# Natural-order normalised rows with strided TensorE transposes, and the last weight split of each attention half placed behind its softmax

## The chip, the cores and the metric

The kernel runs on one core of one Trainium2 chip. The metric is device time in microseconds (us) from the start to the end of one execution; the median of several executions is quoted. Everything is one launch, with all arithmetic on the core.

## What is computed

Two pre-norm residual layers over 512 tokens of width 1024, in float32. Each layer is a token mixer (layer 0 a gated short convolution, layer 1 attention with three dilated windows and rotary positions) followed by a mixture of 16 experts. Cut to what the change touches:

```python
hn = rms_norm(h, norm_mix[i])                      # y = x * rsqrt(mean(x*x) + eps) * g
h = h + mixer(hn)                                  # layer 0: conv, layer 1: attention
hn = rms_norm(h, norm_ffn[i])
h = h + hierarchical_moe(hn, ...)                  # top-1 of 4 groups, then top-2 of 4 experts
# expert e:  silu(t @ w_gate[e]) * (t @ w_up[e]) @ w_down[e]
return rms_norm(h, norm_final)
```

## The kernel before

**Tiles.** The 512 tokens stand in `h` as four row tiles `r` of 128 tokens (partitions) by 1024 channels. A product needs the channels on the partitions, so every normalised row tile is turned by TensorE into eight 128x128 tiles (`k` = 0 to 7) in PSUM. Tile `k` holds the channels 8q + k, q being the partition, because the weights are loaded with the pattern `(p k) n -> p k n`: partition p then reads eight neighbouring rows of the weight matrix in one piece.

**Precision by splitting.** Each operand is split into a high part (ScalarE copies it to the type fp32r) and a low part (VectorE subtracts the high part from the original), and each product is three matmuls, hi*hi, hi*lo and lo*hi (`product`, L298 to L300). Weights come as units of 1 MB. The projections outside the experts use three landing buffers `raw` and two pairs `W_hi`/`W_lo`; in ScalarE's code `hi(u)` (L592) and in VectorE's code `lo(u)` (L816) split unit `u`. The experts use six landing buffers `m_raw` and three pairs (L623, L982).

**Stages on TensorE.** `turn_rows` (L1275) turns the four normalised row tiles, 4 x 8 transposes. It runs four times: before the convolution's projections, before the router of layer 0, before attention's projections, and before the router of layer 1. Around it VectorE runs `norm_row` (L849: hn = h * rstd * gain) and `turn_lo` (L855), ScalarE runs `square` (L598) and `turn_hi` (L603), and GpSimd makes rstd (L470, L471). `norm_row` is used a fifth time for the output.

**Experts.** The normalised rows are also stored to the DRAM tensor `hn_rows`. For each expert item (a block of up to 128 tokens of one expert) GpSimd gathers 128 rows into `x_rows`, `turn_x` (L1348) turns them with eight transposes, and then come four gate/up units of 12 matmuls each and two down units of 12. `turn_x(i + 1)` stands between the gate/up and the down units of item i.

**The permutation.** In the kernel before, `norm_row` writes hn with its channels permuted: it reads `h` and `gain` at a step of eight elements and writes `hn` in one piece, so that the columns of tile k lie side by side:

```python
o = hn[r % 2][:, :].rearrange("p (k q) -> p k q", k=KD)
i0 = h[:, r, :].rearrange("p (q k) -> p k q", k=KD)
rows = hn_r[r % 2][:, k * P:(k + 1) * P]           # turn_rows, and x_rows_r alike in turn_x
```

`pe.transpose(out, rows, ident_r)` loads `rows` as the stationary operand (the row PEld in the profile is this load) and streams the identity.

**Attention.** Two halves `s` of eight heads each. A half projects q, k and v of three head groups `g` (units 0 to 5 of each group, `p` = 0, 1, 2 for q, k, v), and then `attend(s)` runs 16 units `u` (four pairs of heads by four query tiles): scores on TensorE (L1471, L1474), mask and row minimum on VectorE (L1161), exponential on ScalarE (L729), transposes of the probabilities (L1486), their copy back (L1173), weighted sum (L1500). Behind the 16 units VectorE computes the merge scales (`scales`, L1180 to L1190), with one ScalarE exponential in the middle (L762); in half 1 TensorE spreads them (L1454) between the row tiles of the output projection's first unit, VectorE merges (L1199 to L1201) and splits (L1206), and the projection's second unit waits for the last of these splits.

**Order.** Every engine's order is written out by hand. Splits run two units ahead, so while TensorE runs the last unit of group 2, ScalarE and VectorE have one split left to do, `hi(U_QKV + 7)` and `lo(U_QKV + 7)`. It can't begin before TensorE has left the buffer, and in the kernel before it stands right ahead of `attend(s)` on both engines. SyncE issues all weight loads in one queue; a load waits for the low split that frees its buffer.

Of the kernel before, what the change touches and what calls it, by code (L numbers as in the profile page):

```python
# [23 lines left out]
ALU = mybir.AluOpType  # L24
# [32 lines left out]
def build(nc, x, positions, norm_mix, norm_ffn, norm_final, conv_w_in, conv_w, conv_w_out, attn_w_qkv,  # L57
# [19 lines left out]
    with ExitStack() as ctx:  # L77
# [85 lines left out]
        stat_sum = keep("stat_sum", [P, 2, NT, 8])  # L163
        head_scale = keep("head_scale", [P, 2, NT, 8])
        cos_t = keep("cos_t", [P, NT, HD])
        sin_t = keep("sin_t", [P, NT, HD])
# [160 lines left out]
        def _(sp):  # L327
# [95 lines left out]
            store_rows(4)  # L423
            norm_gain(2)
            for j in range(3):
                qkv_unit(j, 0, 0)
            later_weights(0)
            y_back(0)
# [159 lines left out]
        def _(act):  # L588
# [161 lines left out]
            def attend(s):  # L750

                act.wait_ge(qkT_ready, s * 24 + 24 + 4)
                softmax_exp(0, s)
                for u in range(16):
                    if u + 1 < 16:
                        softmax_exp(u + 1, s)
                    if u % NT == 0 and u:
                        store_heads(u // NT - 1, s)
                    if s == 1 and u in (2, 6):
                        heads_hi(u // 4)  # L760
                act.wait_ge(gap_in, s + 1)
                act.activation(stat_exp[:, :, :, :], stat_exp[:, :, :, :], ACT.Exp).then_inc(gap_out, 1)  # L762
                store_heads(3, s)

            for s in range(2):
                for g in range(NATT):
                    for p in range(3):
# [13 lines left out]
                        if p == 2:  # L781
                            for r in range(NT):
# [6 lines left out]
                                else:  # L789
                                    act.activation(v_all[:, g, r, :], ps[:, r, :], ACT.Copy).then_inc(v_ready, 1)  # L790
                        hi(U_QKV + 2 * p + 3, rev)
                attend(s)
# [12 lines left out]
        def _(dve):  # L805
# [26 lines left out]
            def norm_row(k, first, r):  # L832
# [3 lines left out]
                if r >= 2:  # L836
# [4 lines left out]
                    if first == 16:  # L841
                        dve.wait_ge(out_stored[r % 2], 16)
                if first < 16:
                    o = hn[r % 2][:, :].rearrange("p (k q) -> p k q", k=KD)
                    i0 = h[:, r, :].rearrange("p (q k) -> p k q", k=KD)
                    i1 = gain[:, :].rearrange("p (q k) -> p k q", k=KD)
                else:
                    o, i0, i1 = hn[r % 2][:, :], h[:, r, :], gain[:, :]
                dve.scalar_tensor_tensor(out=o, in0=i0, scalar=rstd[:, r:r + 1], in1=i1, op0=ALU.mult,  # L849
                                         op1=ALU.mult).then_inc(hn_ready, 1)  # L850

# [358 lines left out]
            def attend(s):  # L1210

                dve.wait_ge(qkT_ready, s * 24 + 24 + 4)
                mask_scores(0, s)
                for u in range(16):
                    if u + 1 < 16:
                        mask_scores(u + 1, s)
                    probs_back(u, s)
                    if s == 1 and u in (4, 8):
                        heads_lo(u // 4 - 1)
                scales(s)  # L1220

            def rope(g4, rev, p):
# [14 lines left out]
            for s in range(2):  # L1237
                for g in range(NATT):
                    for p in range(3):
# [4 lines left out]
                        if p < 2:  # L1244
                            rope((s * 6 + g * 2 + p) * 4, rev, p)
                        lo(U_QKV + 2 * p + 3, rev)
                        if s == 1 and g == 0:
# [20 lines left out]
        def _(pe):  # L1268
            def turn_rows(first):

                for r in range(NT):
                    pe.wait_ge(hn_ready, first + r + 1)
                    for k in range(KD):
                        rows = hn_r[r % 2][:, k * P:(k + 1) * P]
                        ins = pe.transpose(ps_r[:, 2 * r + k // 4, (k % 4) * P:(k % 4 + 1) * P], rows, ident_r[:, :])  # L1275
# [63 lines left out]
            def experts(l):  # L1339
# [5 lines left out]
                def turn_x(i):  # L1345
                    pe.wait_ge(s["rows_in"], i * 16 + 16)
                    for k in range(KD):
                        ins = pe.transpose(ps_r[:, 2 + k // 4, (k % 4) * P:(k % 4 + 1) * P],  # L1348
                                           x_rows_r[:, k * P:(k + 1) * P], ident_r[:, :])
                    ins.then_inc(s["turned"], 1)  # L1350
# [232 lines left out]
```

## Time and profile before

| | |
|---|---|
| median of 3 runs | 1548.24 us (1543.72 to 1548.25) |
| the profiled execution | 1546.9 us, of which the span from first to last instruction is 1545.2 us |
| mean granted TensorE clock | 0.941 of full |
| TensorE matmuls (PE) busy | 88% |
| TensorE weight loads (PEld) busy | 72% |
| VectorE (DVE) busy | 63% |
| ScalarE (ACT) busy | 49% |
| DRAM traffic | 302 MB, mean 195 GB/s |

The busy time of matmuls is modelled by the profiler and overlaps from one to the next, so a TensorE at 88% is not at 88% of its peak. How fast it goes is read from the starts of neighbouring instructions. The profile names the streamed operand first and the stationary one second: `ps<-ident_r,hn_r` streams the identity and has hn as weights.

### The profile page before, as it was taken

To read this page: it belongs to the slowest core of one execution; us is meant where nothing else is said; L and a number is where in the kernel's file an instruction comes from. 1 tells how busy PE (TensorE), PEld (TensorE's weight loads), DVE (VectorE), ACT (ScalarE), POOL (GpSimd) and SP (SyncE) were. 2 spreads that over 40 slices of the span, in tenths; PEclk is the share of its full clock that TensorE was granted. 3 is DMA by queue.
4 is the path that set the end of the run, shared out by engine and by line. 5 is a ranking of instruction groups with operands and counts; after the bars stand their busy time and mean duration, and the time that the engine had idled before them with its cause. 6 is when DMAs were issued, how large, how long until landed. Compare 5 with 4: busy or idle time off the path is not lost.

```text
span 1545.2 us, 20454 instructions
## 1 busy us (share of the span) xinstructions
PE 1363.3 (88%) x7161; PEld 1119.1 (72%) x7161; DVE 977.9 (63%) x1196; ACT 751.1 (49%) x835; POOL 203.7 (13%) x301
## 2 busy tenths in 40 slices
PE   5999955999999929999988999998886599999991
PEld 4888734888888718888867888887774488888870
DVE  6445364999999773252456535246736489899983
ACT  4222142788888631422264142226513278878871
POOL 4000011111111121120200202020001111111112
PEclk9999976999999959999999999999998699999995
DMA  6232354999999552223210222320044289999964
GB/s 207 82 122 95 123 198 145 348 385 390 390 390 392 227 208 88 90 87 109 82 56 1 82 82 82 101 91 28 1 177 171 80 327 392 392 386 389 391 254 174
DMA packets 83596, 301.94 MB, mean 195 GB/s; under 512 B 12091, under 2 KB 12115, under 8 KB 67156
## 3 DMA queue, kind: packets, MB, share of 16 engines
q1 hardware_dynamic: 74036, 283.86, 49.7%
q0 software_dynamic: 9504, 17.33, 2.9%
q8 instruction: 36, 0.59, 0.1%
q14 instruction: 20, 0.16, 0.0%
HBM read 293.28 MB, written 25.17 MB: 206 GB/s over the span
## 4 chain that ended last, share of the span: by engine, by line
PE 84%; DVE 7%; ACT 3%; DMA 2%; issue 2%; POOL 1%; POOLq 0%; SPq 0%; DVEq 0%; ACTq 0%
PE ps L298 25%; PE ps L300 24%; PE ps L299 24%; PE ps L1500 2%; PE ps L1348 1%; DVE hn L849 1%; PE ps L1486 1%; PE ps L1550 1%; PE ps L1454 1%; DMA x_rows<-hn_rows,tok_list 1%; ACT prob L729 1%; DVE probT L1173 1%; PE ps L1305 1%; ACT square_out L598 1%; PE ps L1471 1%
## 5 line engine op out<-in xcount | busy, mean ns | idle before, releaser
L298 PE MATMUL ps<-W_hi,xT_hi_all 128*128 128x512 f32 x1408 | 561.8, 399 | 18.7 <-DVE xT_lo_all L990 9.6
L300 PE MATMUL ps<-W_hi,xT_lo_all 128*128 128x512 f32 x1408 | 553.3, 393 | 0.0
L299 PE MATMUL ps<-W_lo,xT_hi_all 128*128 128x512 f32 x1408 | 552.4, 392 | 0.0
L982 DVE TENSOR_TENSOR W_lo<-m_raw,W_hi 128x2048 fp32r<-128x2048 f32 x192 | 435.6, 2291 | 65.2 <-ACT W_hi L623 65.2
L623 ACT ACTIVATE W_hi<-m_raw 128x2048 fp32r<-128x2048 f32 x192 | 367.0, 1914 | 45.7 <-PE ps L300 44.7
L816 DVE TENSOR_TENSOR W_lo<-raw,W_hi 128x2048 fp32r<-128x2048 f32 x56 | 135.1, 2414 | 312.3 <-ACT W_hi L592 312.2
L298 PEld LDWEIGHTS ps<-W_hi,xT_hi_all 128*128 128x128 f32 x1408 | 266.7, 189 | 77.1 <-issue 7.3
L300 PEld LDWEIGHTS ps<-W_hi,xT_lo_all 128*128 128x128 f32 x1408 | 266.8, 189 | 57.9
L299 PEld LDWEIGHTS ps<-W_lo,xT_hi_all 128*128 128x128 f32 x1408 | 267.4, 190 | 52.7
L592 ACT ACTIVATE W_hi<-raw 128x2048 fp32r<-128x2048 f32 x56 | 107.1, 1914 | 369.0 <-PE ps L300 367.9
L572 POOL TENSOR_TENSOR qk_rot<-rope_a,rope_b 128x512 f32<-128x512 f32 x48 | 61.8, 1290 | 399.4 <-DVE rope_b L1234 399.2
L640 ACT ACTIVATE xT_hi_all<-ps 128x1024 fp32r<-128x1024 f32 x34 | 34.9, 1027 | 86.8 <-PE ps L1348 83.9
L298 PE MATMUL ps<-xT_hi_all,W_hi 128*128 128x512 f32 x192 | 76.1, 397 | 0.0
L299 PE MATMUL ps<-xT_lo_all,W_hi 128*128 128x512 f32 x192 | 75.7, 394 | 0.0
L300 PE MATMUL ps<-xT_hi_all,W_lo 128*128 128x512 f32 x192 | 75.7, 394 | 0.0
L1275 PE MATMUL ps<-ident_r,hn_r 128*128 128x128 f32 x128 | 19.3, 323 | 60.6 <-DVE hn L849 60.6
L1275 PEld LDWEIGHTS ps<-ident_r,hn_r 128*128 128x128 f32 x128 | 16.4, 177 | 64.0 <-DVE hn L849 54.2
L1231 DVE TENSOR_TENSOR rope_a<-ps,cos_t 128x512 f32<-128x512 f32 x48 | 33.0, 688 | 40.6 <-PE ps L300 39.2
L598 ACT ACTIVATE square_out<-h 128x1024 f32<-128x1024 f32 x20 | 21.1, 1057 | 76.6 <-DVE h L1031 39.8
L470 POOL TENSOR_SCALAR msq<-ssq 128x1 f32<-128x1 f32 x20 | 10.8, 539 | 354.2 <-ACT square_out L598 354.1
L990 DVE TENSOR_TENSOR xT_lo_all<-ps,xT_hi_all 128x1024 fp32r<-128x1024 f32 x34 | 41.3, 1214 | 18.0 <-ACT xT_hi_all L640 18.0
L1173 DVE COPY probT<-ps 128x512 f32<-128x512 f32 (+1 forms) x64 | 39.2, 653 | 14.4 <-PE ps L1486 13.5
(207 smaller groups left out, 1333.4 us busy)
## 6 DMA issues: line engine op xcount, KB each, us to landing
m_raw<-in_w_gate_dram SPq DMA_DIRECT2D x64, 1024.0 KB, 7.8
m_raw<-in_w_up_dram SPq DMA_DIRECT2D x64, 1024.0 KB, 8.6
m_raw<-in_w_down_dram SPq DMA_DIRECT2D x64, 1024.0 KB, 8.4
raw<-in_attn_w_qkv_dram SPq DMA_DIRECT2D x36, 1024.0 KB, 5.0
raw<-in_conv_w_in_dram SPq DMA_DIRECT2D x12, 1024.0 KB, 5.1
y_pick<-y_rows SPq DMA_DIRECT2D x16, 512.0 KB, 7.4
raw<-in_conv_w_out_dram SPq DMA_DIRECT2D x4, 1024.0 KB, 5.0
hn_rows<-hn SPq DMA_DIRECT2D x8, 512.0 KB, 2.6
```

Of the source, the lines that this page charges most:

```text
L298: pe.matmul(o, a_hi, b_hi, start=first, stop=False)
L299: pe.matmul(o, a_hi, b_lo, start=False, stop=False)
L300: return pe.matmul(o, a_lo, b_hi, start=False, stop=last)
L572: pool.tensor_tensor(qk_rot[:, r, :], rope_a[r % 2][:, :], rope_b[r % 2][:, :], ALU.add).then_inc(rope_added, 1)
L592: act.activation(W_hi[uc % SPLIT][:, :, :], raw[uc % RAW][:, :, :], ACT.Copy).then_inc(split_hi, 1)
L598: act.activation(square_out[:, :], h[:, r, :], ACT.Square, accum_out=ssq[:, r:r + 1]).then_inc(ssq_ready, 1)
L623: act.activation(MW_hi[c % MSPLIT][:, :, :], m_raw[c % MRAW][:, :, :], ACT.Copy).then_inc(s["hi"], 1)
L816: dve.tensor_tensor(W_lo[uc % SPLIT][:, :, :], raw[uc % RAW][:, :, :], W_hi[uc % SPLIT][:, :, :].bitcast(F), ALU.subtract).then_inc(split_ ...
L982: dve.tensor_tensor(MW_lo[c % MSPLIT][:, :, :], m_raw[c % MRAW][:, :, :], MW_hi[c % MSPLIT][:, :, :].bitcast(F), ALU.subtract).then_inc(s[ ...
L990: dve.tensor_tensor(xT_lo_all[:, 0:2, :].rearrange("p a n -> p (a n)"), ps[:, 2:4, :].rearrange("p a n -> p (a n)"), xT_hi_all[:, 0:2, :]. ...
L1173: dve.tensor_copy(probT[u % 2][:, hd, k0:S], ps[:, 4 + hd, k0:S]).then_inc(pt_ready, 1)
L1275: ins = pe.transpose(ps_r[:, 2 * r + k // 4, (k % 4) * P:(k % 4 + 1) * P], rows, ident_r[:, :])
```

## The change

Three edits.

1. `norm_row` reads `h` and `gain` and writes `hn` in natural order in all five places. The eight transposes of `turn_rows` and of `turn_x` take their 128 columns at a step of eight elements (32 bytes) instead. The rows in DRAM are in natural order too.
2. `hi` and `lo` of unit `U_QKV + 7` leave the place ahead of `attend(s)`. On ScalarE the split stands behind the half's last softmax exponential and ahead of the one in the scales; on VectorE it stands behind `scales(s)`. A one-element exponential into a new tile `exp_of_half` is issued in group 2 of each half, between the copies of q and the next split.
3. SyncE issues the three loads of the first attention units behind all expert loads of layer 0 rather than ahead of them.

```diff
@@ sync @@
             norm_gain(2)
+            later_weights(0)
             for j in range(3):
                 qkv_unit(j, 0, 0)
-            later_weights(0)
             y_back(0)
@@ scalar, attend @@
+                hi(U_QKV + 7, s * 3 + 2)
                 act.wait_ge(gap_in, s + 1)
                 act.activation(stat_exp[:, :, :, :], stat_exp[:, :, :, :], ACT.Exp).then_inc(gap_out, 1)
@@ scalar, projections of a half @@
-                        hi(U_QKV + 2 * p + 3, rev)
+                        if g == 2 and p == 1:
+                            act.activation(exp_of_half[:, :], neghalf[:, :], ACT.Exp)
+                        if g < 2 or p < 2:
+                            hi(U_QKV + 2 * p + 3, rev)
                 attend(s)
@@ vector, norm_row @@
-                if first < 16:
-                    o = hn[r % 2][:, :].rearrange("p (k q) -> p k q", k=KD)
-                    i0 = h[:, r, :].rearrange("p (q k) -> p k q", k=KD)
-                    i1 = gain[:, :].rearrange("p (q k) -> p k q", k=KD)
-                else:
-                    o, i0, i1 = hn[r % 2][:, :], h[:, r, :], gain[:, :]
-                dve.scalar_tensor_tensor(out=o, in0=i0, scalar=rstd[:, r:r + 1], in1=i1, op0=ALU.mult,
-                                         op1=ALU.mult).then_inc(hn_ready, 1)
+                dve.scalar_tensor_tensor(out=hn[r % 2][:, :], in0=h[:, r, :], scalar=rstd[:, r:r + 1],
+                                         in1=gain[:, :], op0=ALU.mult, op1=ALU.mult).then_inc(hn_ready, 1)
@@ vector, attend @@
                 scales(s)
+                lo(U_QKV + 7, s * 3 + 2)
@@ vector, projections of a half @@
-                        lo(U_QKV + 2 * p + 3, rev)
+                        if g < 2 or p < 2:
+                            lo(U_QKV + 2 * p + 3, rev)
@@ tensor, turn_rows @@
-                        rows = hn_r[r % 2][:, k * P:(k + 1) * P]
+                        rows = hn_r[r % 2][:, k::KD]
@@ tensor, experts, turn_x @@
-                                           x_rows_r[:, k * P:(k + 1) * P], ident_r[:, :])
+                                           x_rows_r[:, k::KD], ident_r[:, :])
```

How ScalarE's order moves at the entry to the softmax of half 0 (`qkT`: copies of k; `v_all`: copies of v; `W_hi_53<-raw_58`: the split of unit U_QKV + 7; `prob`: the exponentials). Before:

```order
L592 ACTIVATE W_hi_53<-raw_56 128x2048
L592 ACTIVATE W_hi_52<-raw_57 128x2048
L780 ACTIVATE qkT<-ps 128x4x128 x4
L790 ACTIVATE v_all<-ps 128x512 x4
L592 ACTIVATE W_hi_53<-raw_58 128x2048
L729 ACT_TABLE_LOAD
L729 ACTIVATE prob_100,near_stat<-prob_100,near_stat 128x128
```

Changed:

```order
L794 ACT_TABLE_LOAD
L794 ACTIVATE exp_of_half<-neghalf 128x1
L593 ACTIVATE W_hi_53<-raw_56 128x2048
L593 ACTIVATE W_hi_52<-raw_57 128x2048
L782 ACTIVATE qkT<-ps 128x4x128 x4
L792 ACTIVATE v_all<-ps 128x512 x4
L730 ACTIVATE prob_100,near_stat<-prob_100,near_stat 128x128
```

The split and the table load no longer stand between the last copy of v and the first exponential; the table load stands a weight unit earlier, ahead of two splits.

VectorE behind the softmax of half 1 (`head_scale`: the last step of the scales; `near_o`, `far_o`: the first merge). Before:

```order
L1189 RECIPROCAL stat_min<-stat_min 128x32
L1190 TENSOR_TENSOR head_scale<-stat_exp,stat_min 128x64
L1199 TENSOR_TENSOR near_o_107<-ps,near_o_107 128x512
L1200 TENSOR_TENSOR far_o_109<-ps,far_o_109 128x512
L1201 TENSOR_TENSOR near_o_107<-near_o_107,far_o_109 128x512
```

Changed:

```order
L1188 RECIPROCAL stat_min<-stat_min 128x32
L1189 TENSOR_TENSOR head_scale<-stat_exp,stat_min 128x64
L821 TENSOR_TENSOR W_lo_55<-raw_58,W_hi_53 128x2048
L1198 TENSOR_TENSOR near_o_107<-ps,near_o_107 128x512
L1199 TENSOR_TENSOR far_o_109<-ps,far_o_109 128x512
```

The low split now stands between the scales and the first merge.

## Rows read from the trace of the kernel before

**Rows 1.** The page: busy time of the engines, and granted clock in 40 slices.

```profile
PE 1363.3 (88%) x7161; PEld 1119.1 (72%) x7161; DVE 977.9 (63%) x1196; ACT 751.1 (49%) x835; POOL 203.7 (13%) x301
...
PEclk9999976999999959999999999999998699999995
```

**Rows 2.** Busy time by stretch: most of layer 0's experts (columns: us, busy and count by engine, clock, DMA).

```profile
281.60:509.70 228.10, 228.10 (x1098) 188.27 (x1097) 207.70 (x118) 186.06 (x130) 37.57 (x52) 1.00 1.00 387
```

**Rows 3.** Timeline of TensorE around one `turn_x`: start us, us, instruction.

```profile
263.86 0.39 PE L300 MATMUL ps<-W_hi,xT_lo_all 128*128 128x512 f32 x1
264.08 0.81 PE L1348 MATMUL ps<-ident_r,x_rows_r 128*128 128x128 f32 x8
264.73 0.46 PE L298 MATMUL ps<-W_hi,xT_hi_all 128*128 128x512 f32 x1
```

**Rows 4.** The line of the transposes of `turn_x`: duration ns min/median/max.

```profile
L1348 PE MATMUL ps<-ident_r,x_rows_r x272: 222/249/369, 250.0 to 1495.9; 128*128 128x128 f32 x136
```

**Rows 5.** The line of norm_row, all 20, and of them the last four (unpermuted) in 1509 to 1546 us.

```profile
L849 DVE SCALAR_TENSOR_TENSOR hn<-h,rstd,gain x20: 1280/2056/2136, 7.7 to 1539.5; 128x1024 f32<-128x1024 f32 x20
...
L849 DVE SCALAR_TENSOR_TENSOR hn<-h,rstd,gain 128x1024 f32<-128x1024 f32 x4 | 5.1, 1283 | 1.8 <-POOL rstd L471 1.8
```

**Rows 6.** Lines of three VectorE reductions: 16 elements, 64 contiguous, 64 at a 64-byte step.

```profile
L883 DVE TENSOR_REDUCE m<-fsel x4: 169/170/170, 228.2 to 1197.0; 128x4 f32<-128x16 f32 x4
...
L936 DVE TENSOR_REDUCE slot_f<-e x4: 219/220/221, 234.5 to 1202.4; 128x4 f32<-128x64 f32 x4
...
L921 DVE TENSOR_REDUCE row_count<-used x2: 257/257/257, 231.7 to 1199.2; 128x16 f32<-128x64 f32 x2
```

**Rows 7.** Timeline of the norm stage ahead of layer 0's router.

```profile
204.03 4.10 DVE L849 SCALAR_TENSOR_TENSOR hn<-h,rstd,gain 128x1024 f32<-128x1024 f32 x2
...
209.47 2.24 POOL L471 TENSOR_TENSOR rstd<-msq,neghalf 128x1 f32<-128x1 f32 x1
...
212.35 2.06 DVE L849 SCALAR_TENSOR_TENSOR hn<-h,rstd,gain 128x1024 f32<-128x1024 f32 x1
...
214.47 1.25 PE L1275 MATMUL ps<-ident_r,hn_r 128*128 128x128 f32 x8 [1.86 <-DVE hn L849]
```

**Rows 8.** Timeline of the norm stage ahead of attention: its last row tile.

```profile
572.71 2.06 DVE L849 SCALAR_TENSOR_TENSOR hn<-h,rstd,gain 128x1024 f32<-128x1024 f32 x1
...
574.82 1.25 PE L1275 MATMUL ps<-ident_r,hn_r 128*128 128x128 f32 x8 [2.09 <-DVE hn L849]
```

**Rows 9.** Timeline of the entry to the softmax, half 0.

```profile
783.12 0.64 PE L1474 MATMUL ps<-qkT 64*128 64x128 f32 x8
...
784.55 2.29 DVE L816 TENSOR_TENSOR W_lo<-raw,W_hi 128x2048 fp32r<-128x2048 f32 x1 [10.44 <-ACT W_hi L592]
786.76 0.28 DVE L1161 CUSTOM_DVE_ANT_0 prob<-ps,near_mask 128x128 f32<-128x128 f32 x1
...
787.13 1.28 ACT L729 ACT_TABLE_LOAD   x1 [2.61 <-DVE near_stat L1161]
```

**Rows 10.** Timeline of the entry to the softmax, half 1.

```profile
1054.69 0.64 PE L1474 MATMUL ps<-qkT 64*128 64x128 f32 x8
...
1058.34 0.28 DVE L1161 CUSTOM_DVE_ANT_0 prob<-ps,near_mask 128x128 f32<-128x128 f32 x1
```

**Rows 11.** Timeline behind the softmax: half 0, then half 1.

```profile
843.78 0.23 DVE L1190 TENSOR_TENSOR head_scale<-stat_exp,stat_min 128x64 f32<-128x64 f32 x1
...
851.22 0.39 PE L300 MATMUL ps<-W_hi,xT_lo_all 128*128 128x512 f32 x1
...
1115.17 0.23 DVE L1190 TENSOR_TENSOR head_scale<-stat_exp,stat_min 128x64 f32<-128x64 f32 x1
1117.53 0.69 DVE L1199 TENSOR_TENSOR near_o<-ps,near_o 128x512 f32<-128x512 f32 x1 [2.14 <-PE ps L1454]
```

**Rows 12.** Timeline around the end of layer 0's experts: last expert loads, first attention splits.

```profile
509.12 9.02 SPq L342 DMA_DIRECT2D m_raw<-in_w_down_dram  x4
...
542.53 3.70 ACT L592 ACTIVATE W_hi<-raw 128x2048 fp32r<-128x2048 f32 x2
```

More of the change, by code:

```diff
@@ L164, in build @@
         head_scale = keep("head_scale", [P, 2, NT, 8])
+        exp_of_half = keep("exp_of_half", [P, 1])
         cos_t = keep("cos_t", [P, NT, HD])
```

## The prediction
> **What bounds the kernel now.** I start with the page's busy times: TensorE's matmuls fill 88% of the span, far ahead of VectorE's 63% [rows 1]. So what lengthens TensorE's stream costs in full, and a saving elsewhere counts only where TensorE waits. Next the busy time by stretch: through 228 us of layer 0's experts TensorE is busy all the time at full clock, VectorE for 208 us [rows 2]. Layer 1's experts look the same. The timeline around one `turn_x` shows the pace: the eight transposes start at 264.08 and the next product at 264.73, with no wait on either side [rows 3]. A longer transpose is paid there at once. Outside the experts TensorE waits at the four norm stages, where VectorE, ScalarE and GpSimd hand row tiles along [rows 7, 8], and at the entry to each softmax [rows 9, 10]. Those are the two places where this change can save; the expert stretch is where it can lose.
>
> **Saving at the norm stages.** Reading h and gain at a step of eight takes 2056 ns, the same instruction in natural order 1283 ns [rows 5]; each of 16 `norm_row` gets 0.77 us shorter. How many lie on the path, stage by stage:
> - Start of the kernel: VectorE's chain is held by rstd and by the first weights' arrival, and only one of the four shows: 0.75 us.
> - Ahead of the router, layer 0 [rows 7]. The last `norm_row` starts at 212.35, behind two others that run in one piece from 204.03 to 208.13, an intermediate low split, and a third. The first gets 0.77 us shorter, so its transposes, ScalarE's last square (behind them in its queue) and the last rstd come 0.77 us earlier; the second and third only clear VectorE for it. The last rstd runs 209.47 to 211.71, for as long as VectorE's third `norm_row` runs, and will end about 210.9. The last `norm_row` then runs about 211.0 to 212.3 rather than to 214.41: 2.1 us. Layer 1's router stage has the same pattern: 2.1 us.
> - Ahead of attention the combine feeds the rows and VectorE works without a gap worth naming from the first `norm_row` to the last, which ends at 574.77 with TensorE's transposes right behind [rows 8]. All four count: 3.1 us.
>
> Sum 8.0 us. The fifth use was in natural order already: nothing.
>
> **Saving at the softmax.** In half 0 the scores of the first unit are there at 783.76 (783.12 + 0.64), but VectorE runs the split from 784.55 and masks from 786.76 [rows 9]. Without the split it masks at 783.76: 3.0 us. The exponential then loaded its table for 1.28 us [rows 9]. The changed order has that load a weight unit earlier, where ScalarE waits for TensorE anyway: 1.3 us more. Half 1: scores at 1055.33, mask at 1058.34 [rows 10], 3.0 us, and there was no table load to save. The 16 units hand work round three engines, so I count both shifts in full to the end of each half: 7.3 us.
>
> The moved split costs nothing by the same reading. Half 0: VectorE is free at 844.01, a low split takes 2.29 us, so it is done at 846.3; TensorE wants it behind 851.22 [rows 9, 11]. ScalarE's part falls into its wait for the scales. Half 1: from 1115.40 the split lasts to 1117.69, and the first merge, which waited for TensorE until 1117.53, starts 0.16 us late [rows 11]; the later merges follow TensorE's rows. It also frees `raw` some 60 us later, but the load that waits for this buffer is wanted only two weight units behind the softmax, each of 48 products at 0.23 us. If this cover were gone, each would cost up to 2.3 us.
>
> **The reordered loads: nothing.** The last expert loads are issued by 518.1 and the first attention split runs at 542.53 [rows 12]; three loads of 1 MB fit between, at the 387 GB/s of rows 2 in about 8 us. At the front, TensorE waits for the router, not for expert weights.
>
> **Cost of the strided loads.** This decides the sign, and no row shows TensorE reading at a step. Eight transposes take 0.81 us with the last one 0.249 us long [rows 3, 4]: one starts every (0.81 - 0.25) / 7 = 80 ns. In the norm stages, where TensorE is mostly idle and the granted clock of the slices falls to 0.6 or 0.7 [rows 1], so that part of the time is at 1.2 GHz, it is (1.25 - 0.37) / 7 = 126 ns [rows 7, 4]. Now the bounds for a load of 128 columns at 32-byte steps:
> - Below: nothing more. The load runs beside the matmul ahead of it and part of its time is hidden.
> - VectorE's own pace at such a step. From 16 to 64 contiguous elements a reduction grows by 50 ns, 1.04 ns each; 64 at a step take 37 ns more, 0.58 ns each [rows 6]. That is 1.62 ns for one element that stands alone, 207 ns for 128.
> - Above: the strided `norm_row`, 2056 / 1024 = 2.01 ns per element with two strided inputs [rows 5], 257 ns for 128.
>
> I take 207 ns as the time between two transposes at either clock: one input stream, as a load has, and if memory is what takes the time, TensorE's clock can't shorten it. At full clock that is 127 ns more per load, in the norm stages 81 ns.
>
> The Trainium skill, "Advanced Engine Details and Errata", section SBUF Cachelines, speaks against this change: lines are 16 bytes, at least two hits per line are needed for full speed, and a different line at each access pays. It has no price. `norm_row` agrees with it, 2056 against 1283 ns [rows 5]; for a weight load no row here shows it.
>
> In the experts there are 272 such transposes, 34 groups of 8 [rows 4]. In 32 groups the first load hides behind a product of 0.23 us, so 7 count: 224 x 0.127 = 28.4 us. The first group of each layer runs alone at the lower clock: 16 x 0.081 = 1.3 us. Of the norm stages' 16 groups I count six on the path (the last of each stage, and the first in the two router stages, by the chain above): 48 x 0.081 = 3.9 us.
>
> **Sum.** -8.0 - 7.3 + 28.4 + 1.3 + 3.9 = +18.3 us on the profiled 1546.9, which stands 1.3 us below the median. On the median: **1566.5 us**.
>
> **The rivals.**
> *The load stays hidden* (34%). If TensorE fetches far enough ahead, or in parallel pieces, the step costs nothing and the rest stands: 1548.2 - 15.3 = 1532.9 us, faster. For it: a load's shown duration (the weight loads fill 72% of the span) already overlaps its neighbours, so there is slack in it [rows 1]. Against it: VectorE doesn't hide the step although it takes 1.04 ns for a contiguous element [rows 6] where TensorE's 80 ns for 128 are 0.63. It decides as long as the extra per load is under 15.3 / 288 = 53 ns. The Trainium skill, "TensorE: Matmul & The Clock Gate", section Weight-path perf modes, says that a fast weight load reads four chunks of 32 columns, "packed or strided"; if that is what runs here, this rival is what follows. No run here shows it yet.
>
> *Only the extra is paid* (20%). The load costs VectorE's surcharge, 0.58 ns per column, on top of what it costs now rather than a pace of its own: 74 ns x 288 = 21.3 us, less 15.3: +6.0, 1554 us. Smaller surcharges slide it into no change: half of this case lies there.
>
> *The merges slip* (4%). In half 1 the low split doesn't fit the gap [rows 11], because the softmax ends with VectorE later against TensorE than now; the four merges and the second projection unit all move by 2.3 us. With the forecast's load: 1569 us.
>
> That the change does nothing at the softmax can be ruled out by the order: split and table load have left the entry.
>
> **How the numbers follow.** A measurement of this kernel can tell about 0.3%, 4.6 us, from no change. Forecast case (loads 180 to 260 ns apart) 42%: slower. Hidden 34%: faster. Only the extra 20%: 10 within 4.6 us, 10 slower. Merges slip 4%: slower. Together faster 0.34, same 0.10, slower 0.56. The upper bound, 257 ns: (224 x 0.177 + 64 x 0.131) - 15.3 = +32.7, 1581 us. At 180 ns it is 224 x 0.100 + 64 x 0.054 - 15.3 = +10.6, so the forecast's own range is 1559 to 1583. The whole range has to take in the hidden case at 1532.9 with a few us of uncertainty in its savings: 1529 to 1583.
>
> **What would show it.** The line of `turn_x`: eight transposes in 1.7 us rather than 0.81, the next product 1.5 us behind the first, and the time per expert item up by 0.9 us. If they still start every 80 ns, the forecast is wrong and the hidden case right. `norm_row` at 1.28 us in all 20. First mask within 0.3 us of the first scores, no table load between masks and exponentials; if the mask still starts 3 us late, the softmax term is wrong. In half 1 the first merge within 0.3 us of the end of TensorE's first spread. No wait of ScalarE for a `raw` landing behind layer 0's experts.

## The result, and the profile after

The changed kernel takes **1537.01 us** (median of 5 runs, 1535.63 to 1539.37) against 1547.49 us (1543.72 to 1548.25) for the kernel before: ratio 0.994, 95% interval 0.9925 to 0.9956. Forecast was 1566.5, slower. The time lies in the range (1529 to 1583), but 29.5 us below the forecast and on the other side of the kernel before; the prediction gave a faster kernel 34%. The profiled execution took 1535.63 us, its span is 1533.9 us, 11.3 us under the span of before.

Busy times of the changed kernel, beside [rows 1]:

```profile
PE 1367.5 (89%) x7161; PEld 1127.4 (73%) x7161; DVE 965.8 (63%) x1196; ACT 750.7 (49%) x837; POOL 197.1 (13%) x301
```

TensorE is busy 4 us longer in a span 11 us shorter: its stream got longer in one place and its waits shorter in others. VectorE is down by 12 us, which is 16 times 0.77.

**Experts.** Timeline around a `turn_x` of the changed kernel, beside [rows 3], then the lines of its transposes and of `norm_row` beside [rows 4, 5] (duration ns min/median/max):

```profile
257.74 1.14 PE L1349 MATMUL ps<-ident_r,x_rows_r 128*128 128x128 f32 x8
258.71 0.46 PE L299 MATMUL ps<-W_hi,xT_hi_all 128*128 128x512 f32 x1
```

```profile
L1349 PEld LDWEIGHTS ps<-ident_r,x_rows_r x272: 186/188/194, 244.3 to 1486.4; 128*128 128x128 f32 x136
L1349 PE MATMUL ps<-ident_r,x_rows_r x272: 222/296/373, 244.3 to 1486.4; 128*128 128x128 f32 x136
...
L848 DVE SCALAR_TENSOR_TENSOR hn<-h,rstd,gain x20: 1274/1280/1285, 7.4 to 1528.2; 128x1024 f32<-128x1024 f32 x20
```

The same line of loads in the kernel before:

```profile
L1348 PEld LDWEIGHTS ps<-ident_r,x_rows_r x272: 137/139/183, 250.0 to 1495.8; 128*128 128x128 f32 x136
```

From the first transpose to the next product it is 0.97 us, where [rows 3] have 0.65. One transpose starts every (1.14 - 0.30) / 7 = 120 ns rather than 80. The forecast had 207. TensorE still never waits in the stretch (225.00 of 225 us busy from 275 to 500, as in [rows 2]), so all of it is paid: 0.32 to 0.34 us for each expert item.

**Norm stages.** Ahead of layer 0's router, beside [rows 7]:

```profile
207.51 1.32 PE L1276 MATMUL ps<-ident_r,hn_r 128*128 128x128 f32 x8 [2.36 <-DVE hn L848]
```

At the lower clock the transposes start every (1.32 - 0.37) / 7 = 136 ns (0.37 us is the longest matmul of the line above), against 126 in [rows 7, 4]: 10 ns, not 81. The loads of these stages show why, first in the kernel before, then in the changed one:

```profile
L1275 PEld LDWEIGHTS ps<-ident_r,hn_r x128: 138/182/183, 9.8 to 1184.1; 128*128 128x128 f32 x128
...
L1276 PEld LDWEIGHTS ps<-ident_r,hn_r x128: 185/190/196, 8.8 to 1169.0; 128*128 128x128 f32 x128
```

A contiguous load of a transpose is recorded at 139 ns at full clock and at 182 ns at the lower one; at a step of eight it takes 188 to 190 ns at either. So the step adds some 50 ns to the load at full clock and 8 at 1.2 GHz.

**Softmax entries.** Timeline of half 0, then half 1, beside [rows 9, 10]:

```profile
783.16 0.29 DVE L1160 CUSTOM_DVE_ANT_0 prob<-ps,near_mask 128x128 f32<-128x128 f32 x1 [9.78 <-PE ps L1475]
783.27 0.64 PE L1475 MATMUL ps<-qkT 64*128 64x128 f32 x8
783.55 0.40 ACT L730 ACTIVATE prob<-prob,near_stat 128x128 f32<-128x128 f32 x1 [1.56 <-DVE near_stat L1160]
784.59 0.45 PE L1487 MATMUL ps<-ident_r,prob_r 128*128 128x128 f32 x3 [0.68 <-ACT prob L730]
...
785.85 0.70 PE L1472 MATMUL ps<-qkT 64*128 64x256 f32 x4
...
1048.94 0.29 DVE L1160 CUSTOM_DVE_ANT_0 prob<-ps,near_mask 128x128 f32<-128x128 f32 x1 [9.75 <-PE ps L1475]
```

The mask starts at 783.16, while the last scores (783.27 to 783.91) are still to come; nothing of the split or of a table load is left. The same two places in the kernel before (TensorE's timeline) show what the forecast didn't read:

```profile
789.47 0.62 PE L1486 MATMUL ps<-ident_r,prob_r 128*128 128x128 f32 x3 [4.83 <-ACT prob L729]
...
790.90 1.23 PE L1471 MATMUL ps<-qkT 64*128 64x256 f32 x4
...
1059.76 0.45 PE L1486 MATMUL ps<-ident_r,prob_r 128*128 128x128 f32 x3 [3.55 <-ACT prob L729]
...
1061.19 1.23 PE L1471 MATMUL ps<-qkT 64*128 64x256 f32 x4
```

Four score products take 1.23 us there and 0.70 in the changed kernel: behind the wait of 4.83 us TensorE ran at its lower clock (the granted clock from 790 to 793 was 0.50, 1.2 GHz; in half 1, behind a wait of 3.55 us, it was 0.50 from 1061 to 1064), after the wait of 0.68 us it stayed at full clock.

**Behind the softmax**, half 1, beside [rows 11]:

```profile
1103.29 2.28 DVE L821 TENSOR_TENSOR W_lo<-raw,W_hi 128x2048 fp32r<-128x2048 f32 x1
1103.43 1.97 PE L1455 MATMUL ps<-ident,head_scale 128*64 128x128 f32 x32 [0.63 <-DVE head_scale L1189]
1105.51 0.69 DVE L1198 TENSOR_TENSOR near_o<-ps,near_o 128x512 f32<-128x512 f32 x1
```

The first merge comes 0.1 us behind the end of TensorE's first spread: no slip.

**Where the time went.** Start times of the same TensorE instruction in both traces, changed minus before:

```
place                              difference   in this stretch
end of layer 0's router            -6.0
end of layer 0's experts           +0.3         +6.3
first product of attention         -1.1         -1.4
steady part of half 0              -6.5         -5.4
steady part of half 1              -12.0        -5.5
end of layer 1's router            -15.0        -3.0
late in layer 1's experts          -9.4         +5.6
end of the span                    -11.3        -1.9
```

### The profile page after: what moved, and what is told of

It is laid out like the page before. It is cut to its first block, busy times and chain, and to the rows that moved or that the text cites. A ratio compares the mean times of both kernels' runs of the same rounds, so it can differ in the third digit from the quotient of the medians.

```text
span 1533.9 us, 20456 instructions
## 1 busy us (share of the span) xinstructions
PE 1367.5 (89%) x7161; PEld 1127.4 (73%) x7161; DVE 965.8 (63%) x1196; ACT 750.7 (49%) x837; POOL 197.1 (13%) x301
## 4 chain that ended last, share of the span: by engine, by line
PE 84%; DVE 7%; ACT 3%; DMA 2%; issue 2%; POOL 1%; SPq 1%; POOLq 0%; DVEq 0%; ACTq 0%
PE ps L299 25%; PE ps L301 25%; PE ps L300 24%; PE ps L1349 2%; PE ps L1501 2%; DVE probT L1172 1%; PE ps L1551 1%; PE ps L1455 1%; DMA x_rows<-hn_rows,tok_list 1%; PE ps L1487 1%; ACT prob L730 1%; DVE hn L848 1%; PE ps L1306 1%; ACT square_out L599 1%; DMA y_pick<-y_rows 1%
## 5 line engine op out<-in xcount | busy, mean ns | idle before, releaser
L1349 PEld LDWEIGHTS ps<-ident_r,x_rows_r 128*128 128x128 f32 x272 | 40.1, 189 | 20.9 <-DMA x_rows<-hn_rows,tok_list 18.3
L1349 PE MATMUL ps<-ident_r,x_rows_r 128*128 128x128 f32 x272 | 39.0, 289 | 18.0 <-DMA x_rows<-hn_rows,tok_list 18.0
L989 DVE TENSOR_TENSOR xT_lo_all<-ps,xT_hi_all 128x1024 fp32r<-128x1024 f32 x34 | 41.5, 1222 | 18.0 <-ACT xT_hi_all L641 18.0
```

The lines of the kernel that those rows point to most:

```text
L989: dve.tensor_tensor(xT_lo_all[:, 0:2, :].rearrange("p a n -> p (a n)"), ps[:, 2:4, :].rearrange("p a n -> p (a n)"), xT_hi_all[:, 0:2, :]. ...
```

## The experiments

Unless stated otherwise a kernel's time is compared with runs of the kernel before on the same chip. The kernel before itself scatters over 1541.4 to 1548.9 us.

**The three edits apart.** `rows_only` is the kernel before with this edit alone:

```
+ dve: norm_row for all stages: o, i0, i1 = hn[r % 2][:, :], h[:, r, :], gain[:, :]
+ pe:  rows = hn_r[r % 2][:, k::KD]              (turn_rows)
+ pe:  x_rows_r[:, k::KD]                        (turn_x)
```

> The kernel before with edit 1 alone (natural rows, strided transposes). Theory A (reading off the changed kernel's trace: a group of eight strided transposes lasts 0.97 us rather than 0.63, 32 such groups stand in the experts, and the norm stages give back about 8 to 10 us): +10.9 us of transposes against the norm stages' saving, net within 4 us of the kernel before, 1544 to 1551. Theory B (the strided rows are what made the changed kernel faster, the softmax edit only what was forecast, 7.3 us): 3 us or more faster, 1540 to 1544, with the expert item still at 17.5 us. Group of eight in the experts 0.97 us by A.

`split_only` has only the moved split and the early exponential:

```
+ act: hi(U_QKV + 7, s * 3 + 2)   behind the softmax; same for lo on dve
+ act: if g == 2 and p == 1: act.activation(exp_of_half[:, :], neghalf[:, :], ACT.Exp)
+      if g < 2 or p < 2:  around the split in the projection loop
```

> The kernel before with edit 2 alone (late split and early exponential; rows permuted as before, loads ordered as before). Theory A (the shortened wait at the softmax entry also keeps TensorE at the upper clock level behind it): 11 to 12.5 us faster than before, about 1536. Theory B (only the forecast shifts, 4.3 + 3.0 us): about 1540. First probability transposes of half 0 about 4 us earlier than before, and a further 1.3 to 2.5 us gained within the next four units by A, nothing further by B.

`loads_only` has only `later_weights(0)` ahead of the three `qkv_unit`.

> The kernel before with edit 3 alone (the three attention loads behind all expert loads). Theory A: no change, within 1.5 us of before. Rival: 3 MB at the head of the expert stretch delayed its first loads or the row gather, then up to 2 us faster.

Measured: `rows_only` 1548.11 us, ratio 1.0011 (1.0002 to 1.002); `split_only` 1534.85 us, 0.9931 (0.9916 to 0.9945); `loads_only` 1546.34 us, 1.0005 (0.9995 to 1.0015); the kernel before 1546.41 us. The split carries the whole gain, 11.6 us; the reordered rows give back in the experts what they save outside; the loads do nothing. The sum, -11.6 + 1.7 - 0.1 = -10.0 us, agrees with the 10.5 us between the medians of the changed kernel and the kernel before.

**Which loads pay.** `hybrid` is the changed kernel with rows permuted, and loads contiguous, where experts and router read them:

```
+ if first in (4, 12): the permuted o, i0, i1 in norm_row
+ hn_r[r % 2][:, k * P:(k + 1) * P] if first in (4, 12) else hn_r[r % 2][:, k::KD]
+ x_rows_r[:, k * P:(k + 1) * P]
```

> The changed kernel, but permuted rows and contiguous transposes in the two router stages and in the experts; natural rows and strided transposes only ahead of the convolution and ahead of attention. Theory A: the expert items go back to 17.52 us (about 11 us back over two layers), the two router stages lose the 1 to 2 us each that natural rows gave: 6 to 10 us faster than the changed kernel, 1527 to 1531. Theory B (the experts' longer transposes are covered): no faster than the changed kernel, 1537 or more.

1531.88 us (1531.3 to 1533.04), ratio 0.9912 (0.9898 to 0.9927): about 4 to 5 us better than the changed kernel, less than the 6 to 10 expected, and no kernel that computes the reference was clearly faster. Between its trace and the changed kernel's, TensorE gains 0.33 us per item in the experts, loses 1.8 and 1.9 us at the transposes of the two router stages, where `norm_row` is slow again, and loses 1.6 us behind the last item of each layer, where its clock falls and the changed kernel's does not (more on that below).

**The load by itself.** `steps` computes nothing of the reference: it copies x to the output, and TensorE runs groups of 24 transposes or matmuls that differ only in the step at which an operand is read, with 30 dense matmuls ahead of each to hold the clock.

> A probe that computes nothing of the reference; it copies x to the output. On TensorE alone: 24 transposes each with the stationary operand at steps of 1, 2, 3, 4, 5, 8 and 16 elements, 24 matmuls of 128 columns with the moving operand at steps of 1, 2, 4 and 8, and 24 matmuls of 512 columns with the stationary operand at 1, 8 and 16, each block behind 30 dense matmuls. 
TensorE's timeline of it: L83 reads the stationary operand at step 1, L85 at step 2; L105 and L107 are at steps 1 and 8 under matmuls of 512 columns. The row behind each group shows where it ends:

```profile
21.68 2.16 PE L83 MATMUL ps<-idr,xr 128*128 128x128 f32 x24
23.68 7.08 PE L84 MATMUL ps<-wr,xr 128*128 128x512 f32 x30
30.60 3.43 PE L85 MATMUL ps<-idr,xr 128*128 128x128 f32 x24
33.87 7.07 PE L86 MATMUL ps<-wr,xr 128*128 128x512 f32 x30
...
129.70 5.60 PE L105 MATMUL ps<-wr,xr 128*128 128x512 f32 x24
135.14 6.97 PE L106 MATMUL ps<-wr,xr 128*128 128x512 f32 x30
141.94 6.03 PE L107 MATMUL ps<-wr,xr 128*128 128x512 f32 x24
147.81 6.97 PE L108 MATMUL ps<-wr,xr 128*128 128x512 f32 x30
```

Start to start, divided by 24, a transpose takes 83 ns at step 1, 136 at step 2, 135, 138 and 135 at steps 3, 4 and 5, 129 at step 8 and 132 at step 16. So for these transposes what counts is contiguous or not; among steps of 2 to 16 the size hardly matters. Of the three theories, C (any step but 1) has the right form, with 120 ns for a measured 129 to 138. Why the same step of 8 gives 120 ns inside the kernel is not known. Under 512 columns the load nearly hides: (135.14 - 129.70) / 24 = 227 ns against (147.81 - 141.94) / 24 = 245 at step 8. The moving operand at steps of 1, 2, 4 and 8 (128 columns) gave 109, 116, 117 and 110 ns: almost free at this pace. The Trainium skill, "Advanced Engine Details and Errata", section SBUF Cachelines, was right that a strided read costs, but its rule that two hits on a 16-byte line suffice doesn't hold for this load: at step 2 two elements share a line, and 136 ns is the full price.

The probe leaves one thing open. The groups for the moving operand are plain matmuls, and the first of them (L97) has both operands contiguous; yet it starts one every 109 ns, and its loads are recorded as long as the strided ones of the transposes:

```profile
L97 PEld LDWEIGHTS ps<-wr,xr x24: 187/192/192, 91.2 to 93.8; 128*128 128x128 f32 x24
...
L107 PEld LDWEIGHTS ps<-wr,xr x24: 316/329/335, 141.7 to 147.3; 128*128 128x128 f32 x24
```

Under 512 columns a contiguous load takes 188 ns and one at step 8 329 ns. So 83 ns and 139 ns belong to contiguous transposes, not to every contiguous load; a strided load under plain matmuls of 128 columns was not run.

**Does the clock carry part of the softmax gain?** `fill_entry` is the kernel before with 14 matmuls, whose result nobody reads, behind the first unit's scores of each half; the split stays where it was.

```
+ if u == 0:
+     for n in range(14):
+         pe.matmul(ps[:, 4, :], xT_hi_all[:, 0, 0:P], W_hi[0][:, 0, :], start=True, stop=True)
```

> The kernel before, unchanged but for 14 dummy matmuls (results not used) in each half, which TensorE runs while it waits for the first probabilities. Theory A (the wait lets the clock fall to its lower level, and that costs in the units behind it): first mask as before, the first probability transposes of half 0 as before, but the units behind them at the upper level; 1 to 1.6 us gained in half 0, up to 1.5 us in half 1, together 1.5 to 3 us faster than before, 1543.5 to 1545. Theory B (the clock plays no part): same as before or up to 1 us slower from the dummies that overrun in half 1.

1543.51 us, ratio 0.9981 (0.9972 to 0.9989), 3.4 us under the kernel before, with work added and nothing taken away. The gain is about the expected one, but by the trace all of it comes from half 1. Its timeline, half 0 and then half 1 (L1519 are the added matmuls):

```profile
787.60 3.47 PE L1519 MATMUL ps<-W_hi,xT_hi_all 128*128 128x512 f32 x14
792.50 0.46 PE L1486 MATMUL ps<-ident_r,prob_r 128*128 128x128 f32 x3 [1.43 <-ACT prob L729]
...
793.75 1.22 PE L1471 MATMUL ps<-qkT 64*128 64x256 f32 x4
...
1059.03 3.47 PE L1519 MATMUL ps<-W_hi,xT_hi_all 128*128 128x512 f32 x14
1062.65 0.45 PE L1486 MATMUL ps<-ident_r,prob_r 128*128 128x128 f32 x3 [0.16 <-ACT prob L729]
...
1063.91 0.70 PE L1471 MATMUL ps<-qkT 64*128 64x256 f32 x4
```

In half 1 the filling closes the gap to 0.16 us, the clock stays up, and 2.8 us are gained against the trace of before. In half 0, where the table load makes the gap longer, 1.43 us stay open, the clock falls all the same (1.22 us for the four products) and nothing is gained. So the clock is a real part of the gain. At these entries it stayed up behind open waits of 0.16 and 0.68 us and fell behind 1.43 us and more.

`no_early_exp` is the changed kernel without the early exponential.

> The changed kernel without the early one-element exponential. Theory A: the table load comes back between the first mask and the first exponential of half 0, 1.3 us slower than the changed kernel, 1538.3; half 1 unchanged. Rival: the load is partly covered, or the longer wait also lets the clock fall, then under 0.5 us or over 2 us.

1540.63 us, ratio 0.9963 (0.9949 to 0.9977): 3.3 to 3.6 us above the changed kernel (1537.3 and 1537.01 us, measured on other occasions). Half 0 of it:

```profile
786.39 1.28 ACT L730 ACT_TABLE_LOAD   x1 [1.54 <-DVE near_stat L1158]
...
788.73 0.45 PE L1485 MATMUL ps<-ident_r,prob_r 128*128 128x128 f32 x3 [1.96 <-ACT prob L730]
...
789.99 1.22 PE L1470 MATMUL ps<-qkT 64*128 64x256 f32 x4
```

TensorE's wait is 1.96 us instead of 0.68, as the table load says, and behind it the clock falls: against the changed kernel's trace 1.3 us are lost at the transposes and 1.5 us more in the units behind. In half 1 nothing is lost. The table load of 1.28 us costs twice its length in this wait.

**Can the same be done elsewhere?** `hybrid_fill` adds such matmuls to `hybrid`: 24 ahead of each layer's first `turn_x`, 16 ahead of the second unit of the output projection.

> The kernel hybrid with dummy matmuls (results not used) in two other waits of TensorE: 16 ahead of the output projection's second unit, 24 ahead of the first gathered rows of each layer's experts. Theory A (clock): the products behind each of the three waits start at 0.23 us apart rather than 0.43 for their first 4 to 6 us; 2.5 us each, 5 to 8 us faster than hybrid, 1524 to 1527. Rival: the clock doesn't rise on dummies, or they overrun the waits: no gain, or 1 to 3 us slower than hybrid.

1531.93 us (1528.14 to 1533.5), the same as `hybrid` where 5 to 8 us were expected: a miss. Its timeline ahead of layer 1's first `turn_x`, and the same place in `hybrid`:

```profile
1195.54 8.48 PE L1389 MATMUL ps<-xT_hi_all 128*128 128x512 f32 x24
1204.88 0.87 PE L1358 MATMUL ps<-ident_r,x_rows_r 128*128 128x128 f32 x8 [0.86 <-DMA x_rows<-hn_rows,tok_list]
```

```profile
1203.09 1.26 PE L1355 MATMUL ps<-ident_r,x_rows_r 128*128 128x128 f32 x8 [8.99 <-DMA x_rows<-hn_rows,tok_list]
```

The matmuls began at the lower clock. TensorE was through with them before the gathered rows landed, and the transposes stand where they stood against `hybrid` ahead of the filling (1.6 us later there, 1.8 here). From 1205 to 1213 us the granted clock was 0.79 rather than 0.50, worth 1.5 us; but from 1222 to 1230 it was 0.79 where `hybrid` had 1.00, and the 1.5 us were gone again by 1228. In layer 0 the filling gained nothing either. In the output projection it did what it was meant to; `hybrid_fill`, then `hybrid`:

```profile
1120.86 3.92 PE L1293 MATMUL ps<-xT_hi_all 128*128 128x512 f32 x16
1125.47 0.50 PE L299 MATMUL ps<-W_hi,xT_hi_all 128*128 128x512 f32 x1 [0.69 <-DVE xT_lo_all L1211]
```

```profile
1123.37 0.50 PE L299 MATMUL ps<-W_hi,xT_hi_all 128*128 128x512 f32 x1 [4.53 <-DVE xT_lo_all L1211]
```

The wait ended when it would have ended anyway. Behind it the products kept their 0.23 us, where `hybrid` runs eight of them 0.43 us apart: 1.6 us gained by the traces. The other differences between the two traces, in places that neither filling touches, are as large, so the medians don't show it. Filling a wait paid where it began at full clock and left 0.16 or 0.69 us open; where it began at the lower clock, the clock it raised didn't last through the next waits.

**The load's price inside the kernel, and a layout that avoids it.** `load_alone` is the changed kernel with one line altered, `x_rows_r[:, k * P:(k + 1) * P]` in `turn_x`; columns of x then meet the wrong rows of the experts' weights, with the same instructions.

> The changed kernel with one line altered: turn_x reads contiguous columns, while norm_row stays in natural order. The experts' weights stay in the old order, so the products of the expert stage pair columns with the wrong rows of the weights; every instruction is there and only the read of the load differs. Theory (the step alone costs 0.34 us per group of eight in the experts): 32 groups by 0.34 us = 10.9 us less than the changed kernel, some 1526 us, and the expert item back at 17.5 us. Rival (another reason: in the permuted-rows version it was a changed rhythm of the DMA or of VectorE that made the items shorter): less than 7 us gained, 1530 us or more.

`kp_experts` has besides `w_gate.rearrange("l e (k p) n -> l e p k n", p=P)`, and the same for `w_up`, so that the weights lie in the order that the contiguous load needs.

> The same, and the gate and up weights of the experts are loaded with rows k*128 + p on partition p instead of 8p + k, so that the result is the reference's again. Each partition's piece of a load is then four separate rows of 2 KB instead of 8 KB in one. Theory (the loads move as fast, as the 2 KB rows of the attention weights do in the trace): the same time as the kernel with only the read altered, 1524 to 1528 us, the fastest so far, 4 to 5 us under the version that permutes the rows only ahead of the router. Rival (the DMA engines are busy all through the experts, and smaller pieces make them the bound): each 1 MB load lands later, TensorE waits in the experts, and the time is over 1532 us, possibly far over.

`load_alone` took 1530.99 us, ratio 0.9905 (0.9886 to 0.9924), 6.0 us under the changed kernel where the theory had 10.9; by the medians that is on the rival's side. By the traces it gained 5.0 us in each layer's experts, with the item back at 17.5 us and nothing else altered there, which is the theory's. `kp_experts` took 1541.24 us, 0.997 (0.996 to 0.9981): **10 us slower** than the same kernel with the old layout, so its theory failed. The page's DMA line of `kp_experts` with the landings of the gate weights, and the same two of `load_alone`:

```profile
DMA packets 132748, 301.94 MB, mean 196 GB/s; under 512 B 12091, under 2 KB 12115, under 8 KB 132692
...
m_raw<-in_w_gate_dram SPq DMA_DIRECT2D x64, 1024.0 KB, 12.9
```

```profile
DMA packets 83596, 301.92 MB, mean 197 GB/s; under 512 B 12095, under 2 KB 12119, under 8 KB 67156
...
m_raw<-in_w_gate_dram SPq DMA_DIRECT2D x64, 1024.0 KB, 7.5
```

The same bytes in 59% more packets; from 430 to 530 us the core moves 377 GB/s rather than 386, and TensorE's item takes 18.1 us rather than 17.5. The first items show nothing (the two traces run level up to 381 us); then the buffers that had been filled ahead are used up. The rival named this: the DMA engines are busy all through the experts, as [rows 2] already showed (DMA share 1.00).

**What the gain in the experts becomes.** The traces gave 10 us for the load, the medians 6, so the changed kernel was run again beside `load_alone`.

> The changed kernel itself once more, word for word, beside the version with only turn_x's read altered, so that both share one chip and one set of runs of the kernel before. In the traces the expert stages differ by 5.0 us each, 10 us in all, while the medians, taken on different occasions, differ by 6.0 us; in the traces the missing 4 us lie in stretches where both run the same instructions at different clocks. Theory (this is the scatter of the clock between chips and occasions): the changed kernel here is some 1540 us, 9 to 10 us above the altered one. Rival (the gain in the experts is partly given back by the clock in every execution): it stays at 1537 us, 6 us above.

> As the version with only turn_x's read altered was the first time (columns of x paired with the wrong rows of the experts' weights): 1531 us by both theories. The difference to the changed kernel, run on the same chip, is what counts: 9 to 10 us by the theory, 6 by the rival.

1537.3 us (ratio 0.9954, 0.9937 to 0.9971) and 1529.44 us (0.9904, 0.9887 to 0.9922): 7.9 us apart, between the two theories. The pair's traces show some 10.3 us gained in the experts and 1.6 us given back behind the last item of each layer, 3.2 us in all. Layer 0, the changed kernel and then `load_again`:

```profile
538.08 0.49 PE L299 MATMUL ps<-W_hi,xT_hi_all 128*128 128x512 f32 x1 [2.30 <-DVE xT_lo_all L1001]
538.41 0.40 PE L300 MATMUL ps<-W_lo,xT_hi_all 128*128 128x512 f32 x1
```

```profile
531.63 0.60 PE L299 MATMUL ps<-W_hi,xT_hi_all 128*128 128x512 f32 x1 [2.27 <-DVE xT_lo_all L1001]
532.03 0.63 PE L300 MATMUL ps<-W_lo,xT_hi_all 128*128 128x512 f32 x1
```

The wait is the same, 2.3 us. Behind it the one goes on at full clock; the other runs eight products 0.43 us apart instead of 0.23. All thirteen traces of whole kernels have this wait, of 2.3 to 2.7 us, once in each layer. Counted from TensorE's timelines (the clock fell where seven to nine products behind the wait are 0.43 us apart):

```
load of turn_x      traces                                            clock fell behind the wait
at a step of 8      changed, after_again, rows_only, no_early_exp      0 of 8
contiguous          before, split_only, loads_only, fill_entry,        15 of 18
                    hybrid, hybrid_fill, load_alone, load_again,
                    kp_experts
```

The three exceptions are layer 0 of the kernel before and layer 1 of `loads_only` and `kp_experts`. So this is not mere scatter: the strided load costs some 11 us in the experts and goes together with up to 3.2 us less behind them, as the rival had it. Why the clock stays up behind the longer transposes isn't shown.

## Why the prediction was wrong

- **The step that failed: "I take 207 ns as the time between two transposes at either clock".** It is 120 ns at full clock, 136 at the lower one. The term of the experts was forecast at +28.4 us; 32 groups by 0.34 us are 10.9, and the stretches show 11.9. Spread over the seven loads of a group that the prediction counts, that is 49 ns each, just under the 53 at which the prediction put the turn of sign; from start to start it is 40 ns, and the step from the last transpose to the product behind it grows too. The error was to price one engine's load by another engine's rate: VectorE's 1.62 ns for an element that stands alone became a pace for TensorE. (The surcharge in it, 0.58 ns, is itself weak: the two reductions of [rows 6] differ in their outputs too, 16 against 4.) Nor is the extra the same at both clocks in the way the forecast had it: the strided load's record stays at 188 to 190 ns, but the contiguous one it replaces grows from 139 to 182 at 1.2 GHz, so there is hardly an extra left.
- Of the rivals, *the load stays hidden* named the sign and came within about 4 us of the time, by luck: the load isn't hidden in the experts, and what it costs there was made up by a larger gain at the softmax and other gains of the clock that it doesn't count. A fast weight load that takes a stride without loss, which the prediction offered as its support, is not what these transposes show. *Only the extra is paid* had the mechanism right (a surcharge on the present load) and the size too large: 74 ns for 49 and, at the lower clock, 10.
- **The other strided terms**, +1.3 and +3.9 us at the lower clock: 64 loads by 10 ns are 0.6 us.
- **Softmax, forecast -7.3 us: too small.** -11.6 measured for that edit alone. The masks moved as forecast. What was missing is the clock: a wait of 4.83 or 3.55 us lowers it for the work behind, and the filling and `no_early_exp` show this effect apart. "I count both shifts in full" gave each entry its own length and no more.
- **Norm stages, forecast -8.0 us: -6.8 in this pair of traces, without the clock.** The two router stages came out at 1.8 and 1.9 us (forecast 2.1 each). The start gave 1.7 (0.75), though the other kernels with natural rows have anything from 0.4 to 1.5 there. Ahead of attention 1.4 of 3.1 us came, because of "all four count". VectorE's timeline of the changed kernel shows why:

```profile
563.09 1.28 DVE L848 SCALAR_TENSOR_TENSOR hn<-h,rstd,gain 128x1024 f32<-128x1024 f32 x1
565.30 1.22 DVE L854 TENSOR_TENSOR xT_lo_all<-ps,xT_hi_all 128x1024 fp32r<-128x1024 f32 x1 [0.93 <-ACT xT_hi_all L604]
...
568.96 1.28 DVE L848 SCALAR_TENSOR_TENSOR hn<-h,rstd,gain 128x1024 f32<-128x1024 f32 x1
571.17 1.23 DVE L854 TENSOR_TENSOR xT_lo_all<-ps,xT_hi_all 128x1024 fp32r<-128x1024 f32 x1 [0.93 <-ACT xT_hi_all L604]
```

  Twice the shorter `norm_row` only lengthens the wait behind it: ScalarE does a square and then the high split, and VectorE's low split needs the latter. A chain without gaps on one engine had a second chain just beneath it.
- **Merges, moved split, reordered loads: nothing**, as forecast.
- With the measured terms the prediction's sum is -6.8 - 11.6 + 10.9 + 0.6 = -6.9 us. The remaining 3.6 us are the clock's by the traces: it rises sooner behind the start (1.0 us) and in layer 0's router (1.2 us), and it doesn't fall behind the last expert item of layer 1 (1.5 us). The first two differ as much between other pairs of traces; the third goes with the strided load, as the table above shows.

## What to carry to other kernels

Price an unseen operand pattern by a small probe, not by another engine's rate. For the fp32r transposes here it mattered only whether the stationary operand was contiguous, and a stride cost least under matmuls of 512 columns (18 ns a load) and at the lower clock (10 ns). A wait of some microseconds on TensorE cost its length and then again what the work behind it lost at 1.2 GHz, so shortening it paid more than its length. Before changing a weight layout to make a read contiguous, look whether the DMA engines have any room left: 10 us were lost where the contiguous read had gained 6 to 8.

## What was not expected of the hardware

- A non-contiguous stationary load of an fp32r transpose costs about the same at any step from 2 to 16 (129 to 138 ns per transpose, 83 contiguous); at a step the moving operand costs at most 8 ns per matmul of 128 columns, on top of 109.
- The strided load's shown duration doesn't follow the granted clock (186 to 194 ns over the whole kernel); the contiguous one's does (139 ns at full clock, 182 at the lower one).
- Behind the same wait of 2.3 us the clock fell in some traces and not in others, 1.6 us each time, and it never fell in the four traces whose experts read at a step. No edit aimed at it.
